# Down products of 90 expert blocks in 45 pairs, by Strassen's seven block products

## The reference

```python
def peer_ffn(h, peer_wq, sub_keys1, sub_keys2, peer_u, peer_v):
    ...
    top_s, pos = lax.top_k(cand_s, PEER_TOPK)
    eid = jnp.take_along_axis(cand_i, pos, axis=-1)
    gate = jax.nn.softmax(top_s, axis=-1)
    ...
        a = jnp.einsum('td,tkd->tk', hb, peer_u[eb], preferred_element_type=jnp.float32)
        a = jax.nn.gelu(a, approximate=False)
        return jnp.einsum('tk,tkd->td', (gb * a).astype(hb.dtype), peer_v[eb])
```

## Time and profile before

| | |
|---|---|
| three executions | 957.54, 959.0, 959.24 us (median 959.0) |
| span of the profiled execution, first to last instruction | 954.6 us |
| median less that span | 4.4 us |
| TensorE busy | 947.5 us, 99% of the span |
| VectorE busy | 755.3 us, 79% |
| ScalarE busy | 470.6 us, 49% |
| GpSimd busy | 211.7 us, 22%, none of it after the first 345 us |

### The profile page before, as it was taken

How to read it: one execution, slowest core, us unless ns; L and a number is a source line. 1 busy time by engine, 2 the same in 40 slices (tenths; PEclk the granted TensorE clock), 3 DMA queues, 4 the chain that set the end, 5 groups by cost and what they waited for, 6 DMA issues and landing times.

```text
span 954.6 us, 16415 instructions
## 1 busy us (share of the span) xinstructions
PE 947.5 (99%) x5340; PEld 830.3 (87%) x5340; DVE 755.3 (79%) x1455; ACT 470.6 (49%) x851; POOL 211.7 (22%) x249
## 2 busy tenths in 40 slices
PE   9999999999999999999999999999999999999998
PEld 9998899999999988888888888888888888888887
DVE  5899759999999988888677777777777767767766
ACT  6576544434899964334443443343343344344342
POOL 4074228887877720000000000000000000000000
PEclk9999999999999999999999999999999999999999
DMA  9544138736544467776666666666666665666664
GB/s 280 167 133 132 46 96 302 192 82 215 158 136 132 138 210 241 244 240 225 198 196 179 195 195 180 197 192 183 196 190 185 196 187 186 195 186 190 194 188 145
DMA packets 73593, 174.72 MB, mean 183 GB/s; under 512 B 6208, under 2 KB 39104, under 8 KB 73296
## 3 DMA queue, kind: packets, MB, share of 16 engines
q1 hardware_dynamic: 73120, 172.02, 59.0%
q0 software_dynamic: 288, 2.10, 1.1%
q10 hardware_dynamic: 144, 0.08, 0.0%
HBM read 165.26 MB, written 6.82 MB: 180 GB/s over the span
## 4 chain that ended last, share of the span: by engine, by line
PE 95%; ACT 2%; DMA 2%; DVE 1%; issue 0%; DVEq 0%; POOLq 0%; ACTq 0%
PE psum L2032 37%; PE psum L2012 18%; PE psum L1878 11%; PE psum L2015 9%; PE psum L1578 5%; PE psum L1847 4%; PE psum L1971 3%; PE psum L1594 2%; DMA rr<-big 1%; PE psum L1635 1%; PE psum L1756 1%; PE psum L1839 1%; PE psum L1872 1%; DMA cst<-in_const_dram 0%; ACT big L636 0%; PE psum L1942 0%
## 5 line engine op out<-in xcount | busy, mean ns | idle before, releaser
L2032 PE MATMUL psum<-rr 128*128 128x512 f32 x1536 | 366.0, 391 | 0.0
L2032 PEld LDWEIGHTS psum<-rr 128*128 128x128 f32 x1536 | 287.5, 188 | 59.8
L2012 PE MATMUL psum<-h_all,rr 128*128 128x512 f32 x728 | 260.6, 392 | 0.0
L825 ACT ACTIVATE rr<-raw 128x1024 fp32r<-128x1024 f32 x94 | 99.7, 1061 | 295.4 <-PE psum L2032 294.4
L1294 DVE TENSOR_TENSOR rr<-raw,rr 128x1024 fp32r<-128x1024 f32 x94 | 115.1, 1225 | 125.4 <-ACT rr L825 125.4
L2015 PE MATMUL psum<-h_all,rr 128*128 128x256 f32 x728 | 188.7, 280 | 0.0
L2012 PEld LDWEIGHTS psum<-h_all,rr 128*128 128x128 f32 x728 | 136.6, 188 | 26.8
L2015 PEld LDWEIGHTS psum<-h_all,rr 128*128 128x128 f32 x728 | 136.7, 188 | 7.2
L1878 PE MATMUL psum<-t32s,raw 128*128 128x256 f32 x544 | 124.4, 379 | 0.0
L1203 DVE TENSOR_TENSOR rr<-raw,rr 128x1024 fp32r<-128x1024 f32 x90 | 109.8, 1219 | 1.4 <-ACT rr L706 1.4
L1878 PEld LDWEIGHTS psum<-t32s,raw 128*128 128x128 f32 x544 | 100.2, 190 | 11.9
(11 more groups left out here) (221 smaller groups left out, 1146.6 us busy)
## 6 DMA issues: line engine op xcount, KB each, us to landing
raw<-in_peer_v_dram SPq DMA_DIRECT2D x128, 512.0 KB, 3.5
raw<-in_peer_u_dram SPq DMA_DIRECT2D x127, 512.0 KB, 3.6
big<-in_w_in_dram SPq DMA_DIRECT2D x10, 1024.0 KB, 5.4
big<-in_peer_wq_dram SPq DMA_DIRECT2D x8, 1024.0 KB, 6.1
up_kept<-gel SPq DMA_DIRECT2D x36, 128.0 KB, 3.8
gel<-up_kept SPq DMA_DIRECT2D x34, 128.0 KB, 3.6
big<-in_w_out_dram SPq DMA_DIRECT2D x4, 1024.0 KB, 5.1
rr<-big POOLq DMA_DIRECT2D x2, 1024.0 KB, 9.8
```

The lines of the kernel that those rows point to most:

```text
L825: act.activation(v_sp[s][:, 0, :], v_raw[s], ACT.Copy).then_inc(v_hi, 1)
L2012: return pe.matmul(both, ut[s][:, 0, k, :], ht[:, :, k, :], start=(k == 0), stop=(k == DK - 1))
L2032: i = pe.matmul(psum[:, 4 + 2 * t + n, :], g_sp[:, s, x, t * P:(t + 1) * P], v_sp[s][:, y, n * 512:(n + 1) * 512], start=(first and m == 0 ...
```

## The change

The down products of blocks 36 to 125 are done in 45 pairs, numbered 18 to 62 (`PF` to `PL`). A pair is a 256-deep product: two blocks of experts by two halves of 128 tokens on one side, two blocks by two halves of 512 columns on the other. As a 2 x 2 product of blocks it takes seven block products in place of eight (Winograd's form of Strassen's scheme), each three matmuls of 512 columns. The operands of the seven products are partly sums and differences:

- GpSimd forms four differences and sums of gated activations of 128 columns (`gate_first`, `gate_rest`) and four quarters of differences of `peer_v`, in three instructions of 1024, 512 and 512 columns (`differences`). It also makes one low part of 1024 columns (`second_low`).
- ScalarE makes the high parts of the operands, VectorE the other low parts, and VectorE's `gated_at` now only multiplies.
- The up products are issued as before, but all into one PSUM bank. VectorE adds their halves into SBUF, and TensorE's next up product waits for that addition (`next_up` waits for `a_sum`).
- In the stage before, GpSimd makes the low parts of three blocks of `peer_u` and prepares the operands of the first pairs. Blocks 126 and 127 keep the old form, behind the pairs; the seven accumulators are joined at the end by GpSimd and VectorE.

The core of the diff:

```diff
+PF, PL = EARLY // 2, NK // 2 - 2
...
+            def first_high(p, s):
+                act.wait_ge(ld_p[s], 16 * p + (32 - 16 * PF - 16 * s))
+                act.wait_ge(c_done, turns(p - 1, 1))
+                act.activation(v_a[:, 0], v_pair[s][:, 0:1], ACT.Copy).then_inc(v_hi, 1)
...
+            def pair_round(p, s):
+
+                gelu_at(2 * p + 2, 0)
+                weights_at(2 * p + 4, 0, 16 * p + (32 - 8 * U_FIRST[0] + 16))
+                first_high(p + 1, 1 - s)
+                few_gates(p + 1)
+                late_high(p + 1, 1 - s)
+                gelu_at(2 * p + 3, 1)
+                weights_at(2 * p + 5, 1, 16 * p + (40 - 8 * U_FIRST[1] + 16))
+                early_diff_high(p + 1, 1 - s)
+                rest_gates(p + 1)
+                second_high(p + 1, 1 - s)
+
+            with act.Fori(PF // 2, PL // 2) as i:
                 for s in range(2):
-                    block_v(s, 2 * i + s, False)
-                    block_g(s, 2 * i + s)
-                    block_u(s, 2 * i + (s + 2), 16 * i + u_landed(s + 2, s), False)
...
+            def halves_sum(b, to):
+
+                dve.wait_ge(a_done, b + (1 - EARLY))
+                dve.tensor_reduce(to, psum[:, 0, :].rearrange("p (a t) -> p t a", a=2), AX.X, ALU.add).then_inc(a_sum, 1)
...
+            def late_low(p, s):
+                dve.wait_ge(v_hi, turns(p, 2))
+                dve.tensor_tensor(v_b[:, 1], v_diff[s][:, 2:4], f(v_b[:, 0]), ALU.subtract).then_inc(v_lo, 1)
...
+            def pair_round(p, s):
+
+                dve.wait_ge(p_gsum, 4 * p + (4 - 4 * PF))
+                halves_sum(2 * p + 2, gel[:, 0, :])
+                gated_at(2 * p + 2, 0, gel[:, 0, :])
+                weights_low(2 * p + 4, 0)
+                first_low(p + 1, 1 - s)
+                few_low(p + 1)
+                late_low(p + 1, 1 - s)
+                halves_sum(2 * p + 3, gel[:, 1, :])
+                gated_at(2 * p + 3, 1, gel[:, 1, :])
+                weights_low(2 * p + 5, 1)
+                early_diff_low(p + 1, 1 - s)
+                rest_low(p + 1)
+
+            with dve.Fori(PF // 2, PL // 2) as i:
                 for s in range(2):
-                    expert_block(s, 2 * i + s)
-                    halves_sum(1 - s, 2 * i + (s + 1))
-            expert_block(0, NK - 2, last=True)
...
+            def gate_rest(p):
+
+                pool.wait_ge(d_gate, 2 * p + (2 - 2 * PF))
+                pool.tensor_tensor(g_parts[:, 5], g_parts[:, 2], g_parts[:, 4], ALU.add).then_inc(p_gsum, 1)
+                pool.wait_ge(p_gsum, 4 * p + (2 - 4 * PF))
+                pool.tensor_tensor(g_parts[:, 6], g_parts[:, 5], g_parts[:, 0], ALU.subtract).then_inc(p_gsum, 1)
+                pool.wait_ge(p_gsum, 4 * p + (3 - 4 * PF))
+                pool.tensor_tensor(g_parts[:, 7], g_parts[:, 3], g_parts[:, 6], ALU.subtract).then_inc(p_gsum, 1)
+
+            def differences(p, s, first=False):
+
+                if not first:
+                    pool.wait_ge(v_lo, 3 * p + (EARLY - 3 * PF - 3))
+                pool.wait_ge(ld_p[s], 16 * p + (32 - 16 * PF - 16 * s))
+                v, w = v_pair[s], v_diff[s]
+                pool.tensor_tensor(w[:, 0::2], v[:, 1::2], v[:, 0:2], ALU.subtract).then_inc(p_diff, 1)
+                pool.wait_ge(p_diff, 3 * p + (1 - 3 * PF))
+                pool.tensor_tensor(w[:, 1], v[:, 3], w[:, 0], ALU.subtract).then_inc(p_diff, 1)
+                pool.wait_ge(p_diff, 3 * p + (2 - 3 * PF))
+                pool.tensor_tensor(w[:, 3], v[:, 2], w[:, 1], ALU.subtract).then_inc(p_diff, 1)
+
+            def second_low(p, s):
+                pool.wait_ge(v_hi, turns(p, 4))
+                pool.tensor_tensor(v_d[:, 1], v_pair[s][:, 2:4], f(v_d[:, 0]), ALU.subtract).then_inc(p_vlo, 1)
+
...
+            weights_low(EARLY + 1)
+            gate_first(PF)
+            weights_low(EARLY + 2)
+            gate_rest(PF)
+            weights_low(EARLY + 3)
+            pool.wait_ge(g_lo, 24)
+            differences(PF, 0, True)
+            pool.wait_ge(g_lo, 32)
+            differences(PF + 1, 1, True)
+
+            with pool.Fori(PF // 2, PL // 2 - 1) as i:
+                for s in range(2):
+                    second_low(2 * i + s, s)
+                    gate_first(2 * i + (s + 1))
+                    gate_rest(2 * i + (s + 1))
+                    differences(2 * i + (s + 2), s)
+            second_low(PL - 2, 0)
+            gate_first(PL - 1)
...
+            def third(g, v, bank, first, last):
+
+                for m, (x, y) in enumerate(((0, 0), (0, 1), (1, 0))):
+                    i = pe.matmul(psum[:, bank, :], g[:, x], v[:, y], start=(first and m == 0), stop=(last and m == 2))
+                return i
+
+            def few_products(p, first, last):
+
+                pe.wait_ge(v_lo, 3 * p + (EARLY - 3 * PF + 1))
+                pe.wait_ge(gs_lo, 2 * p + (1 - 2 * PF))
+                third(g_few[:, :, 0], v_a[:, :, 0], 1, first, last).then_inc(c_done, 1)
+                pe.wait_ge(v_lo, 3 * p + (EARLY - 3 * PF + 2))
+                third(g_few[:, :, 1], v_b[:, :, 0], 2, first, last)
+                pe.wait_ge(gs_lo, 2 * p + (2 - 2 * PF))
+                third(g_rest[:, :, 1], v_b[:, :, 1], 6, False, False).then_inc(c_done, 1)
+
+            def rest_products(p, first, last):
+
+                pe.wait_ge(v_lo, 3 * p + (EARLY - 3 * PF + 3))
+                third(g_rest[:, :, 2], v_c[:, :, 0], 3, first, last)
+                if first:
+                    pe.wait_ge(c_ev, 1)
+                third(g_rest[:, :, 3], v_c[:, :, 1], 7, first, last).then_inc(c_done, 1)
+                pe.wait_ge(p_vlo, p + (1 - PF))
+                third(g_rest[:, :, 0], v_d[:, :, 0], 4, False, False)
+                third(g_rest[:, :, 4], v_d[:, :, 1], 5, False, False).then_inc(c_done, 1)
+
+            def next_up(p, s):
+                pe.wait_ge(a_sum, 2 * p + (s + 2 - 2 * PF))
+                up(s, NK)
...
+            with pe.Fori(PF + 1, PL) as p:
+                pe.wait_ge(ut_lo, 2 * p + (0 - EARLY))
+                next_up(p, 0)
+                few_products(p, False, False)
+                pe.wait_ge(ut_lo, 2 * p + (1 - EARLY))
+                next_up(p, 1)
+                rest_products(p, False, False)
...
-            with pe.Fori(EARLY // 2 + 1, NK // 2 - 1) as i:
-                pe.wait_ge(a_gel, 2 * i + (1 - EARLY))
-                up(0, 2 * i + 2)
-                down(0, 2 * i, False, False)
-                pe.wait_ge(a_gel, 2 * i + (2 - EARLY))
-                up(1, 2 * i + 3)
-                down(1, 2 * i + 1, False, False)
-            down(0, NK - 2, False, False)
-            down(1, NK - 1, False, True)
```

More of the change, by code:

```diff
@@ L29 @@
 EARLY, EARLY_TOP = 36, 15
-RING_END = EARLY - 1 - (EARLY - 2) % 3
 ACT_T = 3
@@ L267, in layer @@
         ld_u = [sem(f"ld_u{s}") for s in range(2)]
-        ld_v = [sem(f"ld_v{s}") for s in range(2)]
+        ld_v = [sem(f"ld_v{s}") for s in range(3)]
+        ld_p = [sem(f"ld_p{s}") for s in range(2)]
         ld_h = sem("ld_h")
@@ L486, in _ @@
[L486 to L493, removed]
+                elif b < 3:
+                    load_v(b + 4)
+                elif b == 3:
+                    load_u(EARLY + 2)
+                elif b + 3 < EARLY:
+                    load_v(b + 3)
@@ new lines, in second_high, with few_gates, rest_gates @@
+            def second_high(p, s):
+                act.wait_ge(c_done, turns(p - 1, 4))
+                act.activation(v_d[:, 0], v_pair[s][:, 2:4], ACT.Copy).then_inc(v_hi, 1)
+            def few_gates(p, first=False):
+                if not first:
+                    act.wait_ge(c_done, turns(p - 1, 2))
+                act.wait_ge(p_gsum, 4 * p + (1 - 4 * PF))
+                act.activation(g_few[:, 0], g_parts[:, 0:2], ACT.Copy).then_inc(gs_hi, 1)
+            def rest_gates(p, first=False):
+                if not first:
+                    act.wait_ge(c_done, turns(p - 1, 4))
+                act.wait_ge(p_gsum, 4 * p + (4 - 4 * PF))
+                act.activation(g_rest[:, 0], g_parts[:, 3:8], ACT.Copy).then_inc(gs_hi, 1)
@@ new lines, in _ @@
+                if b == 14:
+                    first_gelu(EARLY + 1)
+                if b == 15:
+                    weights_at(EARLY + 2, 0, u_landed(EARLY + 2, 0))
+                if b == 22:
+                    weights_at(EARLY + 3, 1, u_landed(EARLY + 3, 1))
+                if b == 25:
+                    act.wait_ge(e_up, EARLY)
+                    few_gates(PF, True)
+                if b == 28:
+                    rest_gates(PF, True)
+            act.wait_ge(v_lo, EARLY - 2)
+            first_high(PF, 0)
@@ new lines, in _ @@
+            with pool.Fori(PF // 2, PL // 2 - 1) as i:
+                for s in range(2):
+                    second_low(2 * i + s, s)
[4 more added lines that the diff above has]
+            gate_first(PL - 1)
+            gate_rest(PL - 1)
+            differences(PL, 0)
+            second_low(PL - 1, 1)
```

(16 more changed lines are left out.)

356 lines of the change are left out of this document (214 added, 142 removed).

## The result

The changed kernel takes 1264.28 us in the median of four runs (1263.45 to 1265.6), the kernel before 958.27 us beside it: a ratio of 1.3207, 95% interval 1.3185 to 1.323. The span of its profiled execution is 1263.6 us, 309.0 us more than before.

The account below looks back on a forecast made before the run. The prediction took TensorE's own instructions to bound the kernel before. From 959.0 us it added 254.5, 2 and 2.3 for the pairs, 11 for the stage before and 6 at the end: +276, 1235 us, range 1130 to 1310.

Parts of the forecast that it names:

- the price of a pair: Pair stage: one pair takes 16.7 - 1.7 + 2.1 = 17.1 us, 6.06 more than before; bounds 14.3 and 19.5 us.
- the stage of blocks 0 to 35: Before the pairs: GpSimd's 13 instructions delay VectorE's work, 0.7 us of a delay hidden: +11 us, between 0 and 19.
- the end: After the pairs: GpSimd's six joining additions beside two old down products, five more VectorE additions: +6 us, between 0 and 12.
- exclusion: GpSimd and VectorE instructions with two SBUF inputs each can't overlap; the later waits, only some 0.14 us of its start hidden.
- The sum of both engines' times alone: Pair stage: two-input work per pair, GpSimd 9.04 plus VectorE 7.65 us, 16.69 us in all.
- the stretches between 809.59 and 813.96 us in which neither works on two inputs: Pair stage: between GpSimd's first and second gate sum neither engine can use 2.1 us per pair.
- hidden in handoffs: Pair stage: about a dozen of 17 two-input instructions hide 0.14 us of their start each, -1.7 us per pair.
- The pairs together: All pairs: 42 x 6.06 = +254.5 us, first pair +2, last two rounds +2.3 together.
- Without exclusion: Rival, pair stage: overlap is free, GpSimd's ring of waits takes 13.2 us a pair, about 1060 us; chance 0.06.
- TensorE as the bound: Rival, pair stage: GpSimd's ring closes in 10.35 us, its work below 6.2 us; faster, 934 us; chance 0.05.
- The clock: Rival, pair stage: TensorE's waits lower its clock, at most +435 us at 1.2 GHz; above 1320 us; chance 0.05.

Follow-up runs that it names:

- The first experiment: Changed kernel with VectorE's seven low-part subtractions per pair made one-input additions over an axis of length one, GpSimd untouched: 1096.26 us (one run).

## Why the prediction was right, point by point

The chip's time was 1264 us where 1235 stood, inside the range; the span grew by 309.0 us where 276 was the sum. Two terms were too small, the price of a pair and the stage of blocks 0 to 35. A third, the end, came out partly by luck.

- **The step that decides, exclusion, was right.** Its evidence was two lengthened instructions in the earlier trace rows and one in the earlier trace rows. Lengths in the profile after, the recovery of untouched GpSimd instructions when VectorE's inputs were changed, and the 0.19 against 1.18 us for one column show it. The Trainium skill's rule for VectorE instructions with two SBUF inputs ("SBUF — State Buffer", Who interferes with whom) agrees with the changed kernel and its five variants. The same section says that a VectorE instruction with at most one SBUF input doesn't contend with GpSimd unless it is in a 2-port perf mode, and that `tensor_scalar` can enter such a mode while `tensor_reduce` on trn2 can't. The first experiment's additions agree with that (0.67 us for 512 columns beside GpSimd), and so does VectorE's copy in the stage of blocks 0 to 35: it has one SBUF input, and it was blocked too, as the timeline of that stage below shows. The forecast knew only instructions with two inputs; in the pair stage VectorE has no such copy, so the price of a pair didn't suffer.
- **The price of a pair** was 17.1 us and is 17.62. The sum of both engines' times alone is 16.83 with gate sums at 0.46 and a multiplication at 0.43 (+0.1 on the forecast); the stretches between 809.59 and 813.96 us in which neither works on two inputs add up to 0.49 + 0.52 + 1.21 + 0.07 = 2.3 us (2.1 in the forecast); so 1.5 us are hidden in handoffs and not 1.7.
- **The pairs together**: from the first up product behind block 35, at 468.85 us, to the end of the last block product (twelve matmuls of 0.229 us from 1245.51, so 1248.3), 779.4 us; 45 x 11.04 = 496.8 before; +282.6 where 254.5 + 4.3 = 258.8 stood. Nearly all of the 24 us missing is 42 x 0.52.
- **The stage of blocks 0 to 35** was priced too low: +11 forecast. Its 36 down products and one up product take from 346.94 to 468.85 us, 121.9 us for 101.4 us of matmuls (36 x 2.74 + 2.77), +20.5. From the first down product to the first block product it is 124.7 us, and 107.3 us with GpSimd's instructions one column wide (350.25 to 457.54): 17.4 of the 20.5 us are GpSimd's. The forecast let 0.7 us of each delay be hidden. The timeline of GpSimd and VectorE shows one more thing it left out:

```profile
418.76 3.31 POOL L1715 TENSOR_TENSOR big<-big 128x1024 f32<-128x1024 f32 x1 [1.15 <-DVE rr L1391]
...
419.74 2.61 DVE L1385 TENSOR_TENSOR big<-big,gel 128x256 f32<-128x256 f32 x1
...
422.15 1.34 POOL L1717 TENSOR_TENSOR big<-big 128x512 f32<-128x512 f32 x1
...
422.39 1.25 DVE L1389 TENSOR_SCALAR rr<-big 128x256 fp32r<-128x256 f32 x1
...
423.57 1.27 POOL L1719 TENSOR_TENSOR big<-big 128x512 f32<-128x512 f32 x1
423.67 1.44 DVE L1391 TENSOR_TENSOR rr<-big,rr 128x256 fp32r<-128x256 f32 x1
```

  VectorE gets one instruction through between two of GpSimd's. Its multiplication, its copy and its low part, which the forecast took as one delay, each wait in turn, and together they pass what two buffers hide: TensorE waits here eight times for a low part, 14.0 us together, up to 4.2 us at once. The copy at 422.39 us has one input; it takes 1.25 us where it takes 0.29 alone, and ends 0.15 us after GpSimd's instruction. And in this stage, where TensorE is the bound, the clock does cost time: it is granted at 0.76 from 420 to 430 us, 0.89 in the ten behind and 0.83 from 450 to 460, and with GpSimd's instructions one column wide at 1.00 throughout.
- **The end** was forecast at +6, and the number came out partly by luck. From the end of the last block product, where the first of the last two down products could begin, it takes 15.3 us to the end of the span; before, from the beginning of that down product at 945.7 us, it took 8.9: +6.4. The forecast had GpSimd's six additions outlast the down products. They end at 1253.67 us, before the second down product begins; what they do is block VectorE:

```profile
1250.41 4.58 PE L2227 MATMUL psum<-late_v,rr 128*128 128x512 f32 x12 [1.93 <-DVE gel L1409]
```

  The first down product begins 2.1 us late, behind VectorE's addition of halves; from its beginning to the second's (1255.14 us) are 4.7 us where 2.75 were, at a granted clock of 0.66 from 1250 to 1255 us, which the forecast didn't have in this term. The rest, with VectorE's last additions, takes 8.5 us where it took 6.1.
- **The rivals.** Without exclusion the ring was put at 13.2 us a pair; the first experiment, which comes near to it, has 13.84. TensorE as the bound needed GpSimd's work gone; with it gone the kernel is faster, 942.83 us, against 934 forecast. The clock did fall, to 0.92, but in the pairs of the changed kernel VectorE doesn't wait for TensorE, so there it costs next to nothing; what it costs in the stage before and at the end is a few us. The rival was right about the clock and wrong about the time.

## What to carry to other kernels

Before work is moved to GpSimd, count the instructions on both engines that read two operands from SBUF, and add up their times (16.83 us a pair here, against TensorE's 11.04 before): if that sum is well above the bound engine's period, expect the move to cost time however idle GpSimd was. One-input copies of VectorE from SBUF to SBUF (`tensor_scalar`) belong in the count too; here one took 1.25 us beside GpSimd and 0.29 alone. A sum below the period isn't enough: with next to no exclusion the ring of waits still took 13.84 us. Per instruction, GpSimd's two-input work is the dearer of the two to have in the way (2.39 against 1.22 us for 1024 columns), so with exclusion it can be right to give the busier VectorE more. A scheme that saves matmuls is worth only what its sums and differences leave over: here 0.69 us of TensorE's time per pair was bought with 6.8 us of GpSimd's time for sums and differences (2.39 + 2 x 1.27 + 4 x 0.46).

## What the runs showed of the hardware that was not expected

- The granted clock fell to 0.92 in the pair stage of the changed kernel, where no matmul waited longer than 2.9 us, and to 0.86 in the kernel with the low part on VectorE, where none waited longer than 1.9. Matmuls of 512 columns take 0.63 us in part of a round there and 0.39 in the rest. With waits of TensorE of 1.0 us at most it had stayed at 1.00.
- Two blocked queues take turns. When both engines have two-input instructions ready, each gets one through, then the other does: in the timeline above VectorE, GpSimd, VectorE, GpSimd, none twice in a row.
- A one-input instruction can be blocked too, depending on its kind. VectorE's TENSOR_SCALAR of 256 columns from SBUF to SBUF took 1.24 to 1.26 us the four times that it met a GpSimd instruction of 512 columns at its start (at 422.39, 453.44, 1244.74 and 1251.21 us), ending 0.14 or 0.15 us after it; alone it takes 0.29. With GpSimd's instructions one column wide, all 36 of the stage of blocks 0 to 35 took 0.29 or 0.30.
- An addition over an axis of length one, with an fp32r output, is a one-input pass at VectorE's ordinary rate (1.22 us for 1024 columns), and it doesn't disturb GpSimd.
